# Spare words in front of the two activation buffers and the four feed-forward product buffers

## The reference

```
def swiglu(x, w_gate, w_up, w_down):
    return (jax.nn.silu(x @ w_gate) * (x @ w_up)) @ w_down

for layer in range(2):
    if layer == 1: shared_kv = shared_moba_kv(h, ...)          # h normed @ w_kv
    h = h + 0.5 * swiglu(rms_norm(h), ffn1 weights)            # 1024 -> 2816 -> 1024
    u = rms_norm(h) @ (a_w_in | b_w_in)
    h = h + concat(conv or attention over u, memory attention) @ w_o
    h = h + 0.5 * swiglu(rms_norm(h), ffn2 weights)
# second block: rms_norm(x) @ w_in (9.2k columns), two attentions,
# gated merge through w_a, w_b, w_out, norm, residual
```

## Time and profile before

| | |
|---|---|
| median of 3 executions | 1222.46 us (1222.39 to 1224.54) |
| the profiled execution | 1224.19 us, span of its instructions 1222.9 us |
| TensorE busy | 1201.9 us (98% of the span), 7,423 matmuls |
| VectorE, ScalarE, GpSimd busy | 878.8, 681.9, 63.5 us |
| TensorE share of the chain that ended last | 85% |
| granted TensorE clock, mean | 0.996 of 2.4 GHz |

### The profile page before, as it was taken

The page is one execution under the profiler, slowest core; times in us unless marked ns, Lnnn a source line. Parts: engine busy times, 40 slices in busy tenths (PEclk is TensorE's granted clock), DMA queues, the critical chain, the costliest instruction groups (busy, mean ns, idle before and its releaser), DMA issues.

```text
span 1222.9 us, 18713 instructions
## 1 busy us (share of the span) xinstructions
PE 1201.9 (98%) x7423; PEld 1054.7 (86%) x7423; DVE 878.8 (72%) x1261; ACT 681.9 (56%) x1039; POOL 63.5 (5%) x88
## 2 busy tenths in 40 slices
PE   7999999989999999999999999999999999999998
PEld 6888888857888888888888887988888899889996
DVE  6886856875887766778766667577776677666875
ACT  5766644635565655556554457556555445556463
POOL 5001000100010000000000122000000000000000
PEclk9999999999999999999999999999999999999999
DMA  9866656661676755667655554047665666646450
GB/s 295 267 196 194 182 181 198 202 165 36 195 207 189 201 174 171 197 184 210 202 174 175 169 191 156 21 150 210 190 189 179 187 185 182 195 129 176 138 170 35
DMA packets 205447, 215.36 MB, mean 176 GB/s; under 512 B 9520, under 2 KB 192432, under 8 KB 205232
## 3 DMA queue, kind: packets, MB, share of 16 engines
q1 hardware_dynamic: 202512, 210.10, 57.5%
q10 hardware_dynamic: 2848, 4.06, 1.0%
HBM read 212.20 MB, written 1.93 MB: 175 GB/s over the span
## 4 chain that ended last, share of the span: by engine, by line
PE 85%; DVE 7%; ACT 5%; DMA 2%; issue 1%; SPq 0%; POOL 0%; ACTq 0%; DVEq 0%
PE psum L490 83%; DVE wlo L1844 3%; ACT whi L1234 2%; DVE hT L2048 1%; DMA raw<-in_ffn_w_up 1%; DMA conv_mem<-hc 1%; DMA h<-conv_mem 1%; PE psum L901 0%; ACT x L1306 0%; ACT qn L1546 0%; DVE acc L1911 0%; DVE x L1920 0%; ACT sqb L1296 0%; DVE qk L2405 0%; ACT qT L1607 0%
## 5 line engine op out<-in xcount | busy, mean ns | idle before, releaser
L490 PE MATMUL psum<-x,whi 128*128 128x512 f32 (+1 forms) x2288 | 627.7, 362 | 6.4 <-ACT whi L1336 4.5
L1844 DVE TENSOR_TENSOR wlo<-raw,whi 128x1024 fp32r<-128x1024 f32 (+2 forms) x402 | 472.4, 1187 | 175.3 <-ACT whi L1234 172.6
L1234 ACT CAST whi<-raw 128x1024 fp32r<-128x1024 f32 (+2 forms) x402 | 404.7, 1021 | 154.9 <-PE psum L490 146.0
L490 PEld LDWEIGHTS psum<-x,wlo 128*128 128x128 f32 x1960 | 369.0, 188 | 68.6 <-DVE wlo L1966 0.4
L490 PE MATMUL psum<-x,wlo 128*128 128x256 f32 x1960 | 414.5, 279 | 0.0
L490 PEld LDWEIGHTS psum<-x,whi 128*128 128x128 f32 x2288 | 348.4, 188 | 8.8 <-ACT whi L1336 4.9
L490 PE MATMUL psum<-g,whi 128*128 128x512 f32 x704 | 221.1, 395 | 0.0
L490 PEld LDWEIGHTS psum<-g,wlo 128*128 128x128 f32 x704 | 132.2, 188 | 31.3
L490 PE MATMUL psum<-whi,x 128*128 128x512 f32 (+1 forms) x512 | 143.0, 379 | 0.1
L490 PE MATMUL psum<-g,wlo 128*128 128x256 f32 x704 | 138.3, 278 | 0.0
L490 PEld LDWEIGHTS psum<-g,whi 128*128 128x128 f32 x704 | 107.2, 189 | 0.0
(11 more groups left out here) (308 smaller groups left out, 837.7 us busy)
## 6 DMA issues: line engine op xcount, KB each, us to landing
raw<-in_ffn_w_gate SPq DMA_DIRECT2D x88, 512.0 KB, 4.6
raw<-in_ffn_w_up SPq DMA_DIRECT2D x88, 512.0 KB, 4.3
raw<-in_ffn_w_down SPq DMA_DIRECT2D x80, 512.0 KB, 4.0
raw<-in_w_in SPq DMA_DIRECT2D x52, 512.0 KB, 3.9
raw<-in_w_o SPq DMA_DIRECT2D x16, 512.0 KB, 4.8
raw<-in_a_w_in SPq DMA_DIRECT2D x14, 512.0 KB, 4.6
raw<-in_w_kv SPq DMA_DIRECT2D x16, 384.0 KB, 3.2
raw<-in_w_mem_kv SPq DMA_DIRECT2D x8, 512.0 KB, 3.9
```

The lines of the kernel that those rows point to most:

```text
L490: return pe.matmul(o, l, r, start=start, stop=stop, skip_group_check=True)
L1234: act.copy(held(B.whi[:, i % SPLIT, :], *n), held(B.raw[:, i % RAW, :], *n)).then_inc(*s.hi.now(i))
L1844: dve.tensor_tensor(held(B.wlo[:, i % SPLIT, :], *n), held(B.raw[:, i % RAW, :], *n), held(B.whi[:, i % SPLIT, :], *n).bitcast(F32), ALU.s ...
```

## The change

Six tensors that nobody reads or writes are allocated, one in front of each of the six buffers: 16 and 32 words in front of `x0` and `x1`, and 96, 112, 16 and 32 words in front of `g0` to `g3`. No instruction is added, taken away or moved; the addresses of operands differ. Everything allocated behind `x0` moves too, by 64 bytes behind `x0` and by 192 bytes behind `x1`; the lead of a `g` moves that `g`, its `gr` and its `pr` alone, as that room is freed again.

```
-    B.x = [sb(f"x{i}", [128, 8, 2, S], F32R) for i in range(2)]
+    B.x = []
+    for i, lead in enumerate((16, 32)):
+        sb(f"lead_x{i}", [128, lead])
+        B.x.append(sb(f"x{i}", [128, 8, 2, S], F32R))
...
     def ffn_space(f):
         c = ExitStack()
         F = Space()
+        sb(f"lead_g{f}", [128, (96, 112, 16, 32)[f]], F32, c)
         F.g = sb(f"g{f}", [128, 22, 2, S], F32R, c)
```

## The result

| | before | after |
|---|---|---|
| median of 4 executions each | 1222.92 us (1222.39 to 1224.54) | 1228.82 us (1228.39 to 1229.57) |
| ratio, with its 95% interval | | 1.0041 (1.0025 to 1.0056) |
| the profiled execution, its span | 1224.19, 1222.9 us | 1229.24, 1228.0 us |

What follows compares the result with a forecast made beforehand. The prediction took TensorE's own pace to bound the kernel. Its terms, 5.4 - 1.2 - 1.2 + 0, gave +3.0 us on the median 1222.46, so 1225.5 us, with a range of 1216.5 to 1231.

Steps and rivals of the forecast that it cites:

- What bounds it: Whole kernel: TensorE, busy 98% of the span, sets the time by its own pace, without idle time in the feed-forwards.
- Step 1: 816 x chunks, on `x0` and `x1`: slow from 690.0 ns to g's pace, +5.4 us, between -7.3 and +12.7.
- Step 2: g chunks: `g0` and `g3` reach 690.0 ns, -1.2 us; `g1` and `g2` unchanged; bounds -5.5 and +3.2.
- Step 3: 208 wide `rows_steps` triples, whose stationary x moves: -1.2 us, between -3.7 and +1.0.
- Step 4: 328 `direct` triples, at 340 or 353.3 ns: 0 taken, between -3.3 and +1.0 us.
- Step 5: Identities, masks, attention tiles, `gr` and `pr` that move along: few matmuls, other engines covered by TensorE, 0.
- Rival B: Whole kernel: no change overall, x's loss given back elsewhere or place mattering only for pairs not struck; 1222.5 us, chance 0.25.
- Rival C: `x0` chunks: starting on a 512-byte boundary makes them faster, -5.5 us, 1217 us; chance 0.22.
- Rival D: `x1` and `g2`, at the weights' own place 128: distance of the two reads counts, slower, 1230.5 us; chance 0.13.
- The two reads of TensorE: Weight load beside streamed operand: inferred to hinder each other by their places, from 690 against 697 ns a chunk.

Runs made afterwards that it cites:

- e11: Kernel of before with 16 spare words in front of `whi`, so weights, x and g all move by 64 bytes; 1224.08 us against 1223.26, ratio 1.0006.
- e3: Kernel of before with both weight arrays moved by 64 bytes to 192, x and g left at 448 and 384 modulo 512; 1226.95 us, ratio 1.0027.
- e2: Kernel of before with `g0` to `g3` at 448, 64, 192 and 320 modulo 512, x unmoved; 1222.09 us against 1222.93, ratio 0.9989.
- e5: Kernel of before with the stationary operand in `two_blocks` cut to one word read 128 times; 1226.67 us against 1222.93, one execution.
- e7: Kernel of before with `wlo` alone moved to 192, g at 128, 0, 64, 480; 1231.14 us against 1223.32, one execution.
- e8: Kernel of before with `wlo` alone moved to 256, g at 128, 0, 64, 224; 1234.12 us against 1223.32, one execution.
- e6: Kernel of before with the streamed operand in `two_blocks` cut to one word read 512 or 256 times; 1189.68 us against 1223.32, one execution.
- e4: Changed kernel with other leads: `x0` 480, `x1` 32, g 32, 96, 160, 352 modulo 512; 1239.22 us against 1223.32 for before, one execution.
- e10: Kernel of before with all g at 448 modulo 512, x as before; 1223.10 us against 1223.26, ratio 0.9996.

## Why the prediction came out as it did

- What bounds it: right. It is the pace of TensorE that moved, at a clock of 1.00; in each of the feed-forwards 1 to 3 its idle time is at most 0.1 us in both traces.
- Step 1, the x chunks: right in size, 696.6 and 696.7 ns where g's pace of 696.6 was taken, +5.4 us. The reason given with it, "the streamed buffer's place modulo 128 decides", was wrong: e11 has x at 0 with 690.0 and e3 has x at 448 with 696.7. It gave the right number because the weights stand at a multiple of 128 themselves, so the place and the distance, both modulo 128, agreed in every chunk of the trace of before. That x0's new distance, 128, costs what distance 0 costs was luck: no row of before had a chunk at 128.
- Step 2, g0 and g3: right, 690.0 each, -1.2 us. That g0 would come out at x's pace, since it takes x's old place, was the surest row of the forecast, and it holds under either reason. g3 at 192 was taken as equal because it is an odd multiple of 64. It is equal because 192 and 448 differ by 256; at 64 or 320 it would have been 693.3 (e2).
- Step 3, `rows_steps`: -1.1 us where -1.2 was taken, by luck. It is the sum of two unlike parts: x1, at the very place of the weights, gains 20 ns a triple, x0 2.7.
- Step 4, `direct`: the term that was mis-sized. "0, with both ends kept", -3.3 and +1.0; it measured +2.2. The upper bound took 353.3, the slowest pace that the trace of before contained, for the slowest possible. The new distances have paces of their own, 356.2 and 360.0, that no row of before shows. This term turns +3.0 into +5.3 (the sum by the paces), and the measured +5.0 lies there.
- Step 5, the buffers that move along: 0 stands. The paces give 5.3 us, and the spans differ by 5.1.
- Rival B fell with x's 696.6. Rival C fell: x0 begins on a boundary of 512 and gains nothing, and e11 and after have it there with both paces. Rival D was right in kind and wrong in size: the distance does count, but the stream at the weights' own place (x1, g2) costs no more than at a distance of 128 (x0, g1), 696.7 and not 705.6, and for `rows_steps` it is the fastest of all.
- The two reads of TensorE: the Trainium skill ("SBUF — State Buffer", "Who interferes with whom") gives them independent ports and has TensorE wait for no other engine. e3 and e5 do not agree with the independence: the pace of an unmoved stream changes by 6.7 ns a chunk with the place of what the load reads, and x's and g's difference goes when the load reads one word. The 650 ns that the prediction estimates from the Trainium skill ("TensorE: Matmul & The Clock Gate", "Back-to-back issue gap") was seen nowhere; the nearest is 660.0 with one word streamed. That section gives the formula for a matmul by itself, and says that it does not hold for a stream of loads and matmuls.

What stays open: by what mechanism the distance counts modulo 256; how `whi` and `wlo` at different places interact (e7, e8); what picks one of the two paces that `direct` has at distance 64 and the chunk at 96; and whether the 30 ns that vanish in e6 are the stream's own or arise beside the load, since e5 leaves 693.3 and not 660.

## What to carry to other kernels

Where TensorE is busy without a gap and loads weights for every matmul, read its pace from first start to last start over a count, by buffer: a difference of 1% a chunk is invisible in busy shares and is the whole effect here. Before you move a buffer, write down the place of both operands of each matmul and look which pairs the trace already contains; a rule in one operand's place is not tested while the other stands still, and a pair that the trace lacks can lie outside all paces seen. Keep such a buffer away from distances of 96, 160 and 224 bytes modulo 256 from its weights (702.7 to 706.6 ns a chunk in e4), and keep arrays that take turns as weights at one place modulo 256 (up to 706.7 in e8 where they are not).

## What the runs showed of the hardware that was not expected

- The pace of matmuls with back-to-back loads depends on the distance of streamed and stationary operand modulo 256: 690.0, 693.3 or 696.7 ns for a chunk of 1,536 streamed words at multiples of 64 (e2, e3, e11), and in steps that differ by form: `rows_steps` is fastest (680.0) at the distance at which `direct` is slowest (360.0).
- Distances that are odd multiples of 32 bytes cost more than any multiple of 64 in three cases of four: 706.6 ns a chunk at 96 (700.0 in one stage), 703 at 160, 702.7 at 224, but 693.3 at 32 (e4).
- Two arrays of weights in turn at different places: up to 706.7 ns a chunk (e8).
- With one word streamed over and over a chunk takes 660.0 ns at both distances that were tried, 64 and 0 (e6), 30 ns less than the best layout gives.
- `direct` has two paces at one layout and at the same place of the program: 52 triples at 340.0 ns in before, at 353.3 in e10, with x and weights where they were.
